# The first mixer as one stage, with its row norms applied late

## The chip, the cores and the metric

The kernel runs on one core of one Trainium2 chip. The metric is the device time of one execution in microseconds (us). The chip's engines are named as the profile names them: PE is TensorE (matrix products; PEld its weight loads), DVE is VectorE, ACT is ScalarE, POOL is GpSimd, and SP is the engine whose queue issues the transfers here. They run side by side, each through its own instructions in order, and wait for one another only by semaphores.

## The reference, cut to what matters

The program computes two transformer blocks over 512 tokens of width 1024. The change touches only the first mixer, which is the first thing computed. Everything behind it (the expert feed-forward of the first block, the whole second block) stays as it is.

```
h  = x + hybrid_mixer(rms_norm(x, mix_norm_g), w_in, ..., w_out)

x_lru, g_lru, a_glu, b_glu = split(n @ w_in)            # 4 x 512 columns
xc    = depthwise_conv(x_lru, width 4)
# per direction (forward, backward):
r, i  = sigmoid(block_diag(xc, w_r)), sigmoid(block_diag(xc, w_i))
log_a = 8 * r * log_sigmoid(lambda);  a = exp(log_a)
u     = sqrt(-expm1(2 log_a)) * (i * xc)
h_t   = a_t h_(t-1) + u_t                               # a scan along the tokens
y_lru = (h_fwd + h_bwd) * gelu(g_lru)
glu   = a_glu * sigmoid(b_glu)
c     = depthwise_conv(glu, width 31)
y_conv = silu(group_layer_norm(c))                      # groups of 64 channels
y     = concat(rms_norm(y_lru, beta_lru), rms_norm(y_conv, beta_conv))
out   = y @ w_out
```

## The kernel before, in words

All activations lie transposed, channels on the 128 partitions and the 512 tokens along the row, so that 1024 channels are 8 chunks of 128x512. A weight matrix is read in panels of 128x1024 (512 KB), which give one output chunk each: SP loads a panel into one of four ring slots (L231), ACT copies it half by half to a rounded high part (L240, L242), POOL subtracts to get the low part (L268), and PE sums 24 products of 128x512: high weight by high input (L282), high by low (L283), low by high (L289). Four PSUM banks take the outputs in turn. The same helper is used throughout the program. ACT's split of panel p+1 stands in its queue in front of its work on the output of panel p (`split_next`).

The mixer is a row of blocks of code, with a barrier of all engines between any two of them:

- `start`: SP loads constants, vectors, x and the first four panels of w_in. DVE squares x and sums the squares over the chunks (15 operations, L330 and L332).
- `norm_x`: PE sums over the partitions (L412), ACT takes the root (L400), DVE inverts it (L427) and scales the 8 chunks (L429), ACT rounds them (L448), and POOL and DVE make the low parts (L455).
- `hybrid_branches`, first block: PE multiplies by the 16 panels of w_in in the order x, gelu, glu, sigmoid, and ACT brings each output out of its bank with its function (L663). DVE runs the short convolution (L718, L720) and the product of the gated branch (L729) beside it. Then PE multiplies the 16 gates (L639; ACT's sigmoid L671), and convolves three of the four chunks of the long convolution by 31 products each with a diagonal matrix (L647), which POOL makes (L623) in 8 buffers. Beside it DVE makes the decay from a tanh with a reciprocal (L734 to L741, eight times, once for each chunk and direction), scans (L743, L745), multiplies by the gelu (L749, L752), and only then convolves the fourth chunk itself, 31 taps (L759, L761).
- second block: the group norm of the four convolved chunks (L779 to L808).
- two calls of `rms` (L398 to L455), one for each branch, one behind the other.
- `linear_add`: the 8 panels of w_out, each followed on DVE by the addition to x (L549) and the squares of the new x (L330, L332).

Behind it stand the next `norm_x` and the expert feed-forward, which are not changed.

Of the kernel before, what the change touches and what calls it, by code (L numbers as in the profile page):

```python
# [29 lines left out]
P = 128  # L30
T = 512
# [36 lines left out]
HALF = PANEL // 2  # L68

# [265 lines left out]
def start(m, io, ahead):  # L335
# [4 lines left out]
    with nc.Block() as block:  # L340
        @block.sync
        def _(sp):
            sp.dma_start(m.const[:, :], io["constants"]).then_inc(loaded, 16)
            sp.dma_start(m.vec[:, :], io["vectors"]).then_inc(loaded, 16)
            for k in range(4):
                sp.dma_start(m.x[:, 2 * k:2 * k + 2, :], io["x"][:, 2 * k:2 * k + 2, :]).then_inc(x_loaded[k], 16)
            sp.sem_inc(m.low, SLOTS)
            sp.sem_inc(m.half_low, SLOTS)
            for s, (source, width) in enumerate(ahead):
                load_panel(m, sp, s, s, source, width)  # L350
            sp.wait_ge(loaded, 32)

        @block.vector
        def _(dve):
            for c in range(DC):
                if c % 2 == 0:
                    dve.wait_ge(x_loaded[c // 2], 16)
                add_squares(m, dve, c)
# [8 lines left out]

        @block.scalar
        def _(act):
            split_high(m, act, (0, 0), 0)  # L370
# [192 lines left out]
def hybrid_mixer(m, io, ahead):  # L563

    with ExitStack() as ctx:
        space = Space(m, ctx, "hybrid", 29904)
        lru, conv = hybrid_branches(m, io, space, panels_ahead(io["w_out"]))
        rms(m, lambda c: lru[:, c, :], 0, lambda c: m.v("beta_lru", c), LRU_C4, T, space)
        rms(m, lambda c: conv[:, c, :], LRU_C4, lambda c: m.v("beta_conv", c), LRU_C4, T, space)
    linear_add(m, io["w_out"], ahead)  # L570


def hybrid_branches(m, io, space, ahead):
    nc = m.nc
# [9 lines left out]
    tanh = take(2 * C4, T)  # L584
    gate_i = take(2 * C4, T)
    root = take(2 * C4, T)
    inv = take(2 * C4, T)
# [4 lines left out]
    b_sig = conv  # L592

    side = m.sem("mix_side_loaded")
    first = m.panels
    in_evac = m.sem("mix_in_evacuated")
    lam_exp = m.sem("mix_lambda_exp")
    lam_done = m.sem("mix_lambda_done")
    xc_ready = m.sem("mix_xc_ready")
    glu_ready = m.sem("mix_glu_ready")  # L600
    gate_done = m.sem("mix_gate_products")
    gate_evac = m.sem("mix_gates_evacuated")
    tanh_done = m.sem("mix_tanh_done")
# [3 lines left out]
    conv_done = m.sem("mix_conv_evacuated")  # L607
    V = m.v
    with nc.Block() as block:
        @block.sync  # L610
        def _(sp):
            sp.dma_start(gate_w, io["lru_gates"]).then_inc(side, 16)
            weight_panels(m, sp, io["w_in"], 4 * C4, ahead)
# [3 lines left out]
        def _(pool):  # L617
            split_low(m, pool, 4 * C4)

            for k in range((C4 - 1) * CONF_TAPS):  # L620
                if k >= DIAGS:
                    pool.wait_ge(diag_used, k - DIAGS + 1)
                nc.gpsimd.tensor_scalar(diag[:, k % DIAGS, :], m.const[:, IDENT:IDENT + P],  # L623
                                        V("conf_w", k), None, ALU.mult).then_inc(diag_ready, 1)

        @block.tensor
        def _(pe):
            panel_products(m, pe, 4 * C4)

            pe.wait_ge(side, 16)  # L630
            pe.wait_ge(xc_ready, C4)
            for j in range(4 * C4):
                gate, way, c = j // (2 * C4), j // C4 % 2, j % C4
                if j >= 4:
                    pe.wait_ge(gate_evac, j - 3)
                else:

                    pe.wait_ge(in_evac, 4 * C4)
                nc.tensor.matmul(m.bank[j % 4][:, :], gate_w[:, (way * 2 + gate) * C4 + c, :], xc[:, c, :],  # L639
                                 start=True, stop=True).then_inc(gate_done, 1)  # L640


            pe.wait_ge(glu_ready, C4)
            for k in range((C4 - 1) * CONF_TAPS):
                c, tap = divmod(k, CONF_TAPS)
                pe.wait_ge(diag_ready, k + 1)
                nc.tensor.matmul(m.bank[4 + c][:, :], diag[:, k % DIAGS, :], glu_pad[:, c, tap:tap + T],  # L647
                                 start=(tap == 0), stop=(tap == CONF_TAPS - 1)).then_inc(diag_used, 1)

        @block.scalar  # L650
        def _(act):
            order = m.scalar_order

            order.step(act, nc.scalar.activation(lam[:, 0, :], m.vec[:, VEC["lam"]:VEC["lam"] + 8], ACT.Abs))
            nc.scalar.activation(lam[:, 1, :], lam[:, 0, :], ACT.Exp, scale=-1.0).then_inc(lam_exp, 1)
            kinds = [(x_pad, ACT.Copy, LRU_LEFT), (g_gelu, ACT.Gelu_apprx_tanh, 0), (glu_pad, ACT.Copy, CONF_LEFT),
                     (b_sig, ACT.Sigmoid, 0)]
            for j in range(4 * C4):
                dst, func, left = kinds[j // C4]
                out = dst[:, j % C4, left:left + T]  # L660
                split_next(m, act, first // SLOTS + j // SLOTS, j % SLOTS)
                act.wait_ge(m.used, used_count(first + j))
                order.step(act, nc.scalar.activation(out, m.bank[j % 4][:, :], func))  # L663
                act.sem_inc(m.bank_free[j % 4], 1)
                act.sem_inc(in_evac, 1)
            for j in range(4 * C4):
                gate, way, c = j // (2 * C4), j // C4 % 2, j % C4
                act.wait_ge(gate_done, j + 1)
                dst = tanh if gate == 0 else gate_i
                bias = V("b_rg" if gate == 0 else "b_ig", way * C4 + c)  # L670
# [2100 lines left out]
```

## Time and profile before

| | |
|---|---|
| time, median of 3 runs | 4083.49 us (4082.08 to 4089.62) |
| time of the profiled execution | 4088.65 us |
| its span, first to last instruction | 4086.9 us |
| PE busy | 3698.0 us, 90% |
| DVE, ACT, POOL busy | 2138.9, 1500.0, 1964.1 us |
| mean granted clock of PE | 0.944 of full |

A row of a timeline gives the start, the busy time, the engine, the line of the kernel, the operation, the tile written and those read with their shapes, and how many instructions were merged. Idle time before it and what ended it stand in brackets. All times are us from the start of the span unless marked ns.

### The profile page before, as it was taken

The page shows a single profiled execution, that of the slowest core. Times are in us where ns is not written, and L with a number is a line of the kernel's source. Part 1 is how long each engine was busy: PE and PEld are TensorE (multiplying, and loading weights), DVE is VectorE, ACT ScalarE, POOL GpSimd, SP SyncE. Part 2 cuts the span into 40 slices and gives each one's busy share as a digit, 9 for nine tenths or more (in the row PEclk, how much of TensorE's full clock was granted, in tenths as well). Part 3 has the DMA queues.
Part 4 walks back from the last instruction along what each step waited for, and adds up shares of the span by engine and source line. Part 5 has one row for each costly group of instructions (what it writes and reads, how often), then busy time and mean ns, then how long its engine had stood idle before and what let it go on. Part 6 is the DMA issues. An engine that isn't in the chain of part 4 may idle for free. (4 is left out here: it accounts for less than half of the span.)

```text
span 4086.9 us, 50848 instructions
## 1 busy us (share of the span) xinstructions
PE 3698.0 (90%) x17284; PEld 3080.0 (75%) x17284; DVE 2138.9 (52%) x3369; ACT 1500.0 (37%) x2617; POOL 1964.1 (48%) x1517
## 2 busy tenths in 40 slices
PE   6948999998899999999989885999979998589999
PEld 5526999998899999988867623788758886357887
DVE  4563398874999867653326126433333322654330
ACT  3322455663333333444223303343234422343332
POOL 3624477336788777655424201454435543114444
PEclk9978999999999999999999867999989999689999
DMA  3002355458999989533332200223323334202332
GB/s 114 24 11 82 105 167 164 167 224 318 357 406 405 365 334 344 180 97 98 92 104 85 62 0 23 90 92 94 88 64 95 96 95 94 56 16 87 95 91 91
DMA packets 172652, 569.68 MB, mean 139 GB/s; under 512 B 15457, under 2 KB 58593, under 8 KB 155012
## 3 DMA queue, kind: packets, MB, share of 16 engines
q1 hardware_dynamic: 152244, 427.68, 31.8%
q0 software_dynamic: 20304, 140.78, 9.2%
q8 instruction: 44, 0.72, 0.1%
q14 instruction: 60, 0.49, 0.0%
HBM read 518.33 MB, written 50.07 MB: 139 GB/s over the span
## 5 line engine op out<-in xcount | busy, mean ns | idle before, releaser
L268 POOL TENSOR_TENSOR weight_low<-weight_ring,weight_high 128x512 fp32r<-128x512 f32 x1264 | 1721.5, 1384 | 1731.7 <-ACT weight_high L240 1308.3
L282 PE MATMUL banks<-normed_high,weight_high 128*128 128x512 f32 (+1 forms) x2592 | 973.1, 375 | 85.6 <-PEq L391 43.9
L283 PE MATMUL banks<-normed_low,weight_high 128*128 128x512 f32 (+1 forms) x2592 | 964.8, 372 | 0.0
L240 ACT ACTIVATE weight_high<-weight_ring 128x512 fp32r<-128x512 f32 x632 | 398.8, 631 | 1328.1 <-PE banks L289 1226.1
L282 PEld LDWEIGHTS banks<-normed_high,weight_high 128*128 128x128 f32 x2592 | 496.5, 192 | 160.2 <-issue 76.7
L289 PE MATMUL banks<-normed_high,weight_low 128*128 128x512 f32 (+1 forms) x2592 | 588.6, 368 | 6.8 <-POOL weight_low L268 6.5
L283 PEld LDWEIGHTS banks<-normed_low,weight_high 128*128 128x128 f32 x2592 | 495.6, 191 | 63.9 <-issue 1.5
L289 PEld LDWEIGHTS banks<-normed_high,weight_low 128*128 128x128 f32 x2592 | 473.3, 188 | 71.7 <-POOL weight_low L268 10.5
L242 ACT ACTIVATE weight_high<-weight_ring 128x512 fp32r<-128x512 f32 (+1 forms) x632 | 389.3, 616 | 78.9 <-PE banks L289 77.7
L1740 DVE TENSOR_TENSOR square<-square,banks 128x512 f32<-128x512 f32 x88 | 60.5, 687 | 417.0 <-PE banks L289 415.4
L282 PE MATMUL banks<-parked_high,weight_high 128*128 128x384 f32 x768 | 262.2, 341 | 16.9 <-ACT weight_high L240 11.4
L283 PE MATMUL banks<-parked_low,weight_high 128*128 128x384 f32 x768 | 261.3, 340 | 0.0
L282 PE MATMUL banks<-hidden_high,weight_high 128*128 128x512 f32 x576 | 229.2, 398 | 0.0
L283 PE MATMUL banks<-hidden_low,weight_high 128*128 128x512 f32 x576 | 225.7, 392 | 0.0
L1762 DVE SCALAR_TENSOR_TENSOR residual<-banks,residual 128x512 f32<-128x512 f32 x32 | 22.1, 692 | 380.2 <-PE banks L289 380.2
L1243 DVE SCALAR_TENSOR_TENSOR picked_rows<-picked_rows,banks 128x1024 f32<-128x1024 f32 x128 | 155.5, 1215 | 54.4 <-DMA picked_rows<-in_expert_rows,picked_experts 53.8
L282 PE MATMUL banks<-middle_high,weight_high 128*128 128x512 f32 x448 | 180.3, 403 | 0.0
L283 PE MATMUL banks<-middle_low,weight_high 128*128 128x512 f32 x448 | 176.5, 394 | 0.0
L1249 DVE SCALAR_TENSOR_TENSOR banks<-picked_rows,picked_weight,banks 128x1024 f32<-128x1024 f32 x128 | 164.1, 1282 | 10.1 <-ACT picked_weight L1261 10.1
L282 PEld LDWEIGHTS banks<-parked_high,weight_high 128*128 128x128 f32 x768 | 145.8, 190 | 18.8 <-ACT weight_high L240 9.8
L1232 POOL DMA_INDIRECT picked_rows<-in_expert_rows,picked_experts x128 | 134.5, 1051 | 43.5 <-DVE banks L1249 25.3
L289 PE MATMUL banks<-parked_high,weight_low 128*128 128x384 f32 x768 | 151.9, 340 | 0.0
(360 smaller groups left out, 5666.9 us busy)
## 6 DMA issues: line engine op xcount, KB each, us to landing
weight_ring<-in_experts SPq DMA_DIRECT2D x256, 512.0 KB
weight_ring<-in_ffn_gate SPq DMA_DIRECT2D x88, 512.0 KB
weight_ring<-in_ffn_up SPq DMA_DIRECT2D x88, 512.0 KB
weight_ring<-in_ffn_down SPq DMA_DIRECT2D x64, 512.0 KB
expert_gates<-spread_space SPq DMA_DIRECT2D x6, 4096.0 KB, 12.2
parked_space<-expert_gates SPq DMA_DIRECT2D x24, 768.0 KB
parked_space<-parked_activations SPq DMA_DIRECT2D x24, 768.0 KB
weight_ring<-in_a_w_in SPq DMA_DIRECT2D x28, 512.0 KB
```

The costliest lines, as they stand in the source:

```text
L240: m.nc.scalar.activation(m.w_hi[:, s % PARTS, 0:HALF], m.ring[:, s, 0:HALF], ACT.Copy).then_inc(m.half_high, 1)
L242: m.nc.scalar.activation(m.w_hi[:, s % PARTS, HALF:width], m.ring[:, s, HALF:width], ACT.Copy).then_inc(m.high, 1)
L268: m.nc.gpsimd.tensor_tensor(m.w_lo[:, s % PARTS, at], m.ring[:, s, at], m.w_hi[:, s % PARTS, at].bitcast(FP), ALU.subtract).then_inc(done, 1)
L282: m.nc.tensor.matmul(out, w_hi, hi(c), start=(first and c == 0), stop=False)
L283: m.nc.tensor.matmul(out, w_hi, lo(c), start=False, stop=False)
L289: ins = m.nc.tensor.matmul(out, w_lo, hi(c), start=False, stop=(last and c == chunks - 1))
L1232: m.nc.gpsimd.indirect_dma_start(picked.rows[:, k % ROWS, :], None, io["expert_rows"], bass.IndirectOffsetOnAxis(ap=picked.expert[:, k:k + ...
L1243: m.nc.vector.scalar_tensor_tensor(out=halves[:, 0], in0=halves[:, 0], scalar=1.0, in1=picked.token, op0=ALU.mult, op1=ALU.mult, accum_out ...
L1249: m.nc.vector.scalar_tensor_tensor(out=picked.total, in0=halves[:, 1], scalar=picked.weight[:, k:k + 1], in1=picked.total, op0=ALU.mult, o ...
L1740: nc.vector.tensor_tensor(tile, tile, m.bank[2 * v + 1][:, :], ALU.mult).then_inc(product.sem, 1)
L1762: ins = nc.vector.scalar_tensor_tensor(out=x, in0=m.bank[c % 4][:, :], scalar=0.5, in1=x, op0=ALU.mult, op1=ALU.add)
```

## The change

The mixer becomes one block of code, from the loads to the additions to x.

- `start` keeps only the loads, in another order (vectors, two chunks of x, panel 0, the rest of x, panel 1, constants, panels 2 and 3), and what PE gives to the semaphores. The input of w_in is x times the gain, not yet divided by its norm: ACT rounds x*gain, and DVE makes the low part. DVE squares x behind that, PE sums over the partitions behind panel 1, ACT takes the root, DVE inverts it, and DVE multiplies each output of w_in by it as it takes it out of its bank.
- The panels of w_in come in the order glu and sigmoid of chunks 2, 3, 0, 1, then the four of x, then the four of gelu. ACT applies sigmoid and gelu in place, behind the split of the panel two further on.
- DVE convolves chunks 2 and 3 itself, 31 taps each, in pairs, and chunks 0 and 1 stay on PE (62 products, not 93). 20 of the 31 pairs stand between the outputs of w_in, two at a panel from the fifth on, one at each panel of x.
- The decay comes from an exponential on ACT. DVE's reciprocals and four other operations of each of the eight turns go.
- The steps of the group norm stand between the taps on PE and the recurrences on DVE.
- The two branch norms are late as well: w_out's input is the branch times beta. A half panel of w_out (`half_panel`) gives an output chunk of one branch, DVE multiplies it by that branch's inverse root and adds it to x. So there are 16 half outputs, two to a panel, and w_out is repacked on the host's side of the layout.

```diff
@@ start
         def _(sp):
-            sp.dma_start(m.const[:, :], io["constants"]).then_inc(loaded, 16)
+            sp.sem_inc(m.low, SLOTS)
+            sp.sem_inc(m.half_low, SLOTS)
             sp.dma_start(m.vec[:, :], io["vectors"]).then_inc(loaded, 16)
             for k in range(4):
                 sp.dma_start(m.x[:, 2 * k:2 * k + 2, :], ...).then_inc(x_loaded[k], 16)
+                if k == 0:
+                    load_panel(m, sp, 0, 0, *ahead[0])
             for s, (source, width) in enumerate(ahead):
-                load_panel(m, sp, s, s, source, width)
+                if s:
+                    load_panel(m, sp, s, s, source, width)
+                if s == 1:
+                    sp.dma_start(m.const[:, :], io["constants"]).then_inc(loaded, 16)
@@ hybrid_branches, TensorE
+            for j in range(IN):
+                s = j % SLOTS
+                pe.wait_ge(m.bank_free[s], fill0 + j // SLOTS + 1)
+                ready = (lambda c: pe.wait_ge(x_low, c + 1)) if j == 0 else None
+                part_products(...).then_inc(m.used, 1)
+                if j == 1:
+                    pe.wait_ge(loaded, 32)
+                    pe.wait_ge(prepared.sem, prepared.base + 1)
+                    scale.sums(pe)
...
+            def out_panel(k):
+                banks = [2 * k % SLOTS, 2 * k % SLOTS + 1]
+                for b in banks:
+                    pe.wait_ge(m.bank_free[b], out_fill0 + 2 * k // SLOTS + 1)
+                if k in (0, OUT // 2):
+                    pe.wait_ge(out_low, k + C4 if k else C4)
+                half_panel(m, pe, out_first + k, k % SLOTS, banks, 0 if k < OUT // 2 else C4)
+            gates()
+            taps(0, CONF_TAPS)
+            average(2)
+            average(3)
+            taps(CONF_TAPS, CONF_TAPS + 8)
+            square_sum(2)
+            square_sum(3)
+            taps(CONF_TAPS + 8, CONF_TAPS + 16)
+            average(0)
+            taps(CONF_TAPS + 16, PE_TAPS)
+            square_sum(0)
+            row_sum(0, lru_sq)
+            average(1)
+            out_panel(0)
+            square_sum(1)
+            for k in range(1, OUT // 2):
+                out_panel(k)
+            row_sum(1, sq)
+            for k in range(OUT // 2, OUT):
+                out_panel(k)
@@ hybrid_branches, ScalarE
+            act.wait_ge(loaded, 32)
+            for c in range(DC):
+                if c % 2 == 0:
+                    act.wait_ge(x_loaded[c // 2], 16)
+                nc.scalar.activation(m.n_hi[:, c, :], m.x[:, c, :], ACT.Copy, scale=V("mix_g", c)).then_inc(x_high, 1)
+                if c == 1:
+                    split_high(m, act, (0, 0), 0)
...
+            for j in range(IN + SHAPE_BEHIND):
+                if j < IN:
+                    split_next(m, act, first // SLOTS + j // SLOTS, j % SLOTS)
+                if j == 1:
+                    scale.root(act)
...
+                if j >= SHAPE_BEHIND and HYBRID_ORDER[j - SHAPE_BEHIND][0] in ("gelu", "sigmoid"):
+                    shape(shapes, *HYBRID_ORDER[j - SHAPE_BEHIND])
+                    shapes += 1
...
+            square_centred(2)
+            square_centred(3)
+            root_of(2)
+            root_of(3)
+            split_next(m, act, out_first // SLOTS, 0)
+            lru_input(0)
+            evacuate(0)
+            lru_input(1)
+            square_centred(0)
+            lru_input(2)
+            lru_input(3)
+            root_of(0)
+            evacuate(1)
+            square_centred(1)
+            row_root(0)
+            root_of(1)
@@ hybrid_branches, VectorE
+            for j in range(IN):
+                kind, c = HYBRID_ORDER[j]
...
+                dve.wait_ge(m.used, used_count(first + j))
+                order.step(dve, vec.tensor_tensor(dst, m.bank[j % 4][:, :], m.sum[:, :], ALU.mult))
+                dve.sem_inc(m.bank_free[j % 4], 1)
+                if kind in ("sigmoid", "gelu"):
+                    dve.sem_inc(scaled, 1)
+                if kind == "x":
+                    short_conv(c)
+                if j == 2:
+                    lambdas()
+                if j >= 4:
...
+                    more = 1 if kind == "x" else 2
+                    long_conv(taps, taps + more)
+                    taps += more
...
+            def recur(c):
+                for w in (c, C4 + c):
+                    dve.wait_ge(root_done, ways.index(w) + 1)
+                    order.step(dve, vec.scalar_tensor_tensor(out=root[:, w, :], in0=decay[:, w, :], scalar=1.0,
+                                                             in1=root[:, w, :], op0=ALU.add, op1=ALU.mult))
+                    order.step(dve, vec.tensor_tensor(root[:, w, :], root[:, w, :], gate_i[:, w, :], ALU.mult))
+                    turn = slice(None) if w < C4 else slice(None, None, -1)
+                    order.step(dve, vec.tensor_tensor_scan(gate_i[:, w, turn], decay[:, w, turn], root[:, w, turn], 0.0,
+                                                           ALU.mult, ALU.add))
...
+            def add_out(branch, o):
+                k = branch * OUT // 2 + o // 2
+                done = m.used if o % 2 else m.half_used
+                dve.wait_ge(done, used_count(out_first + k))
+                t = part[:, o % 2, :]
+                order.step(dve, vec.tensor_tensor(t, m.bank[o % 4][:, :], inv[:, branch, :], ALU.mult))
+                dve.sem_inc(m.bank_free[o % 4], 1)
+                order.step(dve, vec.tensor_tensor(m.x[:, o, :], m.x[:, o, :], t, ALU.add))
...
+            centre(2)
+            centre(3)
+            recur(0)
+            normalise(2)
+            recur(1)
+            lru_low(0)
+            normalise(3)
+            recur(2)
+            lru_low(1)
+            centre(0)
+            recur(3)
+            lru_low(2)
+            lru_low(3)
+            normalise(0)
+            centre(1)
+            row_inverse(0)
+            normalise(1)
+            add_out(0, 0)
+            add_out(0, 1)
+            for k, c in enumerate(gln):
+                conv_low(c)
+                add_out(0, 2 + k)
+            add_out(0, 6)
+            add_out(0, 7)
+            row_inverse(1)
+            for o in range(DC):
+                add_out(1, o)
+                add_squares(m, dve, o)
```

## Rows read from the trace of the kernel before

**Rows 1.** Windows by stage: length; busy of PE, PEld, DVE, ACT, POOL; clock, DMA share, GB/s.

```profile
0.00:39.00 39.00, 2.10 (x3) 0.57 (x3) 25.89 (x32) 9.75 (x15) 7.20 (x9) 1.00 0.34 119
39.00:128.40 89.40, 89.40 (x384) 73.57 (x384) 23.40 (x35) 31.20 (x51) 46.96 (x40) 1.00 0.35 106
128.40:143.20 14.80, 13.90 (x33) 6.19 (x33) 0.69 (x1) 10.83 (x16) 0.00 (x0) 1.00 0.00 0
143.20:223.30 80.10, 80.05 (x187) 34.97 (x185) 75.00 (x78) 12.71 (x22) 70.26 (x85) 1.00 0.00 0
223.30:237.40 14.10, 0.00 (x0) 0.00 (x0) 13.42 (x18) 0.68 (x1) 0.00 (x0) 0.67 0.00 0
237.40:262.60 25.20, 9.06 (x16) 3.76 (x16) 18.67 (x12) 9.27 (x14) 0.00 (x0) 0.70 0.00 0
262.60:297.90 35.30, 12.92 (x17) 4.93 (x17) 18.75 (x14) 12.13 (x20) 6.96 (x5) 0.60 0.00 0
297.90:344.20 46.30, 46.30 (x192) 37.75 (x192) 19.38 (x20) 9.73 (x16) 22.77 (x16) 0.94 0.30 91
```

**Rows 2.** Timeline of PE: two products at the low level, the gates, the taps.

```profile
39.53 0.63 PE L283 MATMUL banks<-normed_low,weight_high 128*128 128x512 f32 x1
39.95 0.63 PE L282 MATMUL banks<-normed_high,weight_high 128*128 128x512 f32 x1
...
129.44 13.97 PE L639 MATMUL banks<-hybrid_space 128*128 128x512 f32 x32 [0.90 <-ACTq L665]
143.24 80.01 PE L647 MATMUL banks<-hybrid_space 128*128 128x512 f32 x186
```

**Rows 3.** Timeline of the start, DVE and ACT, and transfers of its first 16 us.

```profile
8.91 0.69 DVE L330 TENSOR_TENSOR residual_squares<-residual 128x512 f32<-128x512 f32 x1 [8.91 <-DMA residual<-in_x]
...
13.98 0.63 ACT L240 ACTIVATE weight_high<-weight_ring 128x512 fp32r<-128x512 f32 x1 [11.60 <-DMA weight_ring<-in_w_in]
...
23.02 3.35 DVE L427 RECIPROCAL norm_space<-norm_space 128x512 f32<-128x512 f32 x1 [3.25 <-ACT norm_space L400]
...
0.00:16.00 16.00, 0.00 (x0) 0.00 (x0) 6.79 (x10) 2.43 (x3) 0.19 (x4) 1.00 0.82 283
```

**Rows 4.** Timeline of DVE, first and last of the tiny operations on lambda.

```profile
40.43 0.85 DVE L701 TENSOR_SCALAR hybrid_space<-hybrid_space 128x8 f32<-128x8 f32 x1 [1.53 <-ACT hybrid_space L655]
...
45.99 0.17 DVE L711 TENSOR_SCALAR hybrid_space<-hybrid_space 128x8 f32<-128x8 f32 x1
```

**Rows 5.** Lines, ns min/median/max: taps beside the low split, alone; POOL's split beside taps.

```profile
L720 DVE SCALAR_TENSOR_TENSOR hybrid_space<-hybrid_space,vectors x12: 737/748/1780, 68.0 to 79.5; 128x512 f32<-128x512 f32 x12
...
L761 DVE SCALAR_TENSOR_TENSOR hybrid_space<-hybrid_space,vectors x30: 751/752/753, 213.7 to 236.6; 128x512 f32<-128x512 f32 x30
...
L268 POOL TENSOR_TENSOR weight_low<-weight_ring,weight_high x6: 1342/1579/1734, 64.9 to 77.3; 128x512 fp32r<-128x512 f32 x6
...
74.18:79.62 5.44, 5.44 (x25) 4.50 (x24) 5.41 (x6) 1.75 (x4) 3.31 (x2) 1.00 0.34 98
```

**Rows 6.** Timeline: ACT's eight tanh; one turn of DVE's recurrence.

```profile
144.23 5.01 ACT L677 ACTIVATE hybrid_space<-hybrid_space 128x512 f32<-128x512 f32 x8
...
159.18 0.68 DVE L740 TENSOR_TENSOR hybrid_space<-hybrid_space 128x512 f32<-128x512 f32 x1
159.90 0.74 DVE L741 TENSOR_TENSOR hybrid_space<-hybrid_space 128x512 f32<-128x512 f32 x1
160.67 1.28 DVE L743 TENSOR_TENSOR_SCAN hybrid_space<-hybrid_space 128x512 f32<-128x512 f32 x1
```

**Rows 7.** Timeline of DVE beside w_out: first addition, a slow sum, the last sum.

```profile
306.16 0.69 DVE L549 TENSOR_TENSOR residual<-residual,banks 128x512 f32<-128x512 f32 x1 [8.89 <-PE banks L289]
307.00 0.87 DVE L330 TENSOR_TENSOR residual_squares<-residual 128x512 f32<-128x512 f32 x1
...
313.34 1.67 DVE L332 TENSOR_TENSOR residual_squares<-residual_squares,square 128x512 f32<-128x512 f32 x1
...
345.88 0.69 DVE L332 TENSOR_TENSOR residual_squares<-residual_squares,square 128x512 f32<-128x512 f32 x1
```

More of the change, by code:

```diff
@@ L68 @@
 HALF = PANEL // 2
+HYBRID_ORDER = [(kind, c) for c in (2, 3, 0, 1) for kind in ("glu", "sigmoid")] + \
+               [(kind, c) for kind in ("x", "gelu") for c in range(LRU_C4)]
 VEC = {}
@@ L566, in hybrid_mixer, with half_panel @@
         space = Space(m, ctx, "hybrid", 29904)
[L567 to L570, printed above, removed]
+        hybrid_branches(m, io, space, ahead)
+def half_panel(m, pe, p, s, banks, chunks):
+    half = HALF // P
+    ready = ((m.half_high, m.half_low), (m.high, m.low))
+    for k in range(2):
+        out = m.bank[banks[k]][:, :]
+        high, low = ready[k]
+        pe.wait_ge(high, p + 1)
+        for c in range(half):
+            w_hi = m.w_hi[:, s % PARTS, (k * half + c) * P:(k * half + c + 1) * P]
+            m.nc.tensor.matmul(out, w_hi, m.n_hi[:, chunks + c, :], start=(c == 0), stop=False)
+            m.nc.tensor.matmul(out, w_hi, m.n_lo[:, chunks + c, :], start=False, stop=False)
+        pe.wait_ge(low, low_count(p))
+        for c in range(half):
+            w_lo = m.w_lo[:, s % PARTS, (k * half + c) * P:(k * half + c + 1) * P]
+            ins = m.nc.tensor.matmul(out, w_lo, m.n_hi[:, chunks + c, :], start=False, stop=(c == half - 1))
+        ins.then_inc(m.used if k else m.half_used, 1)
 def hybrid_branches(m, io, space, ahead):
@@ L583, in hybrid_branches @@
     xc = take(C4, T)
-    tanh = take(2 * C4, T)
+    root = take(2 * C4, T)
     gate_i = take(2 * C4, T)
-    root = take(2 * C4, T)
-    inv = take(2 * C4, T)
+    decay = take(2 * C4, T)
     conv = take(C4, T)
@@ L2704, in layouts @@
     io["x"] = f["x"][0].T.reshape(DC, P, T).transpose(1, 0, 2)
-    io["w_in"] = panels(f["w_in"][0])
-    io["w_out"] = panels(f["w_out"][0])
+    kinds = ("x", "gelu", "glu", "sigmoid")
+    w = panels(f["w_in"][0])
+    io["w_in"] = np.stack([w[kinds.index(kind) * LRU_C4 + c] for kind, c in HYBRID_ORDER])
+    w = panels(f["w_out"][0])
+    io["w_out"] = np.stack([np.concatenate([w[2 * k, :, half], w[2 * k + 1, :, half]], axis=1)
+                            for half in (slice(0, HALF), slice(HALF, PANEL)) for k in range(DC // 2)])
     gates = np.zeros((P, 4 * LRU_C4, P), np.float32)
```

405 lines of the change are left out of this document (240 added, 165 removed).

## The prediction, made before the changed kernel ran

> **What bounds the kernel now.** I read the windows by stage first, because the page's shares (PE 90% busy) are an average over a long program and say little of this stage. [rows 1] shows where the mixer's time lies. Up to 39 us nothing but the first norm runs; PE is busy 2.1 us. From 39 to 128.4 PE is full with w_in. From 143.2 to 223.3 PE is full with taps and DVE is 75 of 80 us busy with the recurrences. Then come four stretches in which PE waits for DVE and ACT: DVE's own 31 taps to 237.4, the group norm to 262.6, two branch norms to 297.9, with PE at 0, 9.1 and 12.9 us. Last come the eight panels of w_out to 344.2. DVE is idle for three quarters of w_in (23.4 of 89.4 us). So the stage is bound by PE and DVE in turn, and most work of one has none of the other beside it. Then I read PE's and DVE's timelines for the price of each operation.
>
> **The units.** A panel of w_in or w_out is 24 products, 5.44 us at full clock by the window of one panel [rows 5]. At the low level (1.2 GHz) two products start 0.42 us apart [rows 2], 10.2 us a panel. A gate or tap is 0.86 us of PE (80.01/93; the 186 records are two a tap) [rows 2]. On DVE a dependent tap costs 0.79 us alone (0.752 busy and some 0.03 for its semaphore), a pair of which only the second is waited for 1.54 [rows 5]; a product of two tiles 0.73 (159.18 to 159.90) [rows 6]; one that takes a bank with its semaphores 0.84 (306.16 to 307.00) [rows 7]; a reciprocal 3.39 [rows 3]. I lay the new code out in the time of the old trace.
>
> **Start.** ACT and DVE wait for the constants, which SP now issues behind six transfers of 512 KB. 283 GB/s over 16 us are 4.5 MB [rows 3], and everything issued is 4.5 MB, the constants end at 3.5 MB of it. Panel 0 landed at 13.98 with 3.0 MB ahead or in it. So the constants land between 12.5 and 16 us; I take 14.5. ACT rounds two chunks and panel 0 (0.55 to 0.6 us each), PE begins at 17.4, and runs one chunk for each low part of DVE (0.78 us) or at the low level, 0.85 us: panel 0 to about 26, panel 1 to 31.5. DVE has its 8 low parts at 23, then 15 squares and sums, 11 us, and 2 us lost to POOL (below): 36. Here the change adds a wait: PE, behind panel 1, stands until 36 for `prepared`, and panels 2 to 15 are queued behind it. The sum over partitions takes 1 to 2 us, so panel 2 starts at 37.5. 14 panels at 5.44 end at 114, where before w_in ended at 128.4: **14 us less**. If the wait of 4.5 us lets the clock fall, panel 2 costs up to 2.7 us more (the first panel of w_out took 8.1 at its low start, 297.9 to 306); if squares and constants are early, it is 4.5 less. DVE's inverse, banks 0 and 1 and the tiny operations on lambda (5.7 us, [rows 4]) are done at 50, before panel 4 ends at 54.
>
> **DVE beside w_in.** From panel 4's end DVE owes, clean: 4.8 us for the fifth output (with two gated products and two pairs), 3.9 or 4.7 for the next three, 6.1 for the first x (0.85, four short taps 2.95, one gated product, one pair), 5.3 for three more, 3.9 for each gelu. Up to the last bank's product it is 52.0 us, and 0.7 of waiting for the sigmoid, which ACT gives only behind the next split. POOL's split takes some away: 12 taps beside it had a median of 748 and a maximum of 1780 ns [rows 5], and six operations filled a panel's 5.44 us, where six clean ones are 4.49. So DVE loses 0.95 us a panel, 10.5 in 11 panels. 63.2 us behind 53.8 the last output is out of its bank, at 117.3, 3.3 behind PE. It never holds PE up, since four banks allow three panels of lag, nor ACT, whose gelu comes two panels behind. Bounds: no loss, 2.8 us earlier; a loss of a whole pair of POOL's operations a panel is a rival.
>
> The Trainium skill (SBUF — State Buffer, "Who interferes with whom") has a rule that speaks against this: GpSimd and a DVE operation with two SBUF inputs hold their shared ports for a whole instruction, and the other blocks fully. By it the 20 pairs would pay up to POOL's full time, as in rival B. The rows agree in kind (1780 against 748) and show less in the mean.
>
> **Gates and taps.** ACT's last gelu and a load of sigmoid's table end near 120, PE has four gates ahead and 12 to go at 0.86: 131, before it was 143.2 (here 2 us of the 14 are given back). DVE's other 11 pairs (17 us) and 8 products end at 144.5, ACT's exponential, tanh and root (8 each at 0.63 [rows 6], and up to three table loads) at 150. Both are hidden, for PE does chunk 0's taps first, 31 x 0.86 = 26.7, to 157.7, and the averages of chunks 2 and 3 stand behind them. DVE is idle from 144.5 to 158.7: this cover costs 14 us of DVE and is late next.
>
> **The DVE chain.** From 158.7 DVE is never free. Two centrings 1.6; four recurrences, each of two turns of 0.82+0.78+1.30 [rows 6] and two products, 7.25, so 29.0; two of the group norm's inversions 4.1 each; three or four low parts and a centring 4. That is 43 us, to 202. The eight turns before were 7.68 us each (61 us), with 31 taps (24) and the norms behind. PE's other 31 taps and sums (34 us) end at 189 under it and then wait.
>
> **Into w_out.** ACT's last branch input, the row sum, chunk 1's average: PE starts w_out at 205, panel 0 at the low level first, 8.1 us: 213. The square sum of chunk 1 stands behind it, its root comes at 214.7, and DVE, which has waited, normalises to 218.8. Then eight additions of branch 0 at 1.57 and four low parts, 15.6, and 2 of POOL's: 236.5. PE in turn waits for banks 0 and 1 (to 221.4, 2 us) and does panels 2 and 3 to 232.4, the row sum 3.4, ACT's root: 236.7. DVE inverts to 240.2. Branch 1 owes 0.84 + 3 x 0.73 = 3.03 us of DVE for each output, against 2.72 of PE: 8 of these less the first sum are 23.5, and 2 for POOL (one sum here took 1.67 and not 0.69 [rows 7]), so **265.7**, 9 us behind PE's last product. DVE, not PE, ends the stage.
>
> **Sum.** Before, the last sum ended at 345.88+0.69 = 346.6. The saving is 346.6-265.7 = 80.9 us; nothing behind it changes. The profiled execution took 4088.65 (span 4086.9), so 4007.8 in its terms. It was 5.2 over the median of the runs, 4083.49, and in the median's terms the time is 4002.6: I predict 4003.
>
> **Rivals.**
> - C, everything is hidden: no wait for the squares (-4.5), no port loss (-2.8 in w_in, -4 behind). 4003-11 = 3992. For it: DVE's taps alone were never slowed (751 to 753). Against: POOL splits in every panel.
> - A, w_out at the low level throughout. For it: PE's clock was 0.60 to 0.70 in all three stretches with gaps [rows 1], and w_out now has gaps of 2 to 4 us. Against: it rose within w_out before. 8 panels at 10.2 from 205, the sums at double price: 296 and 3 for the last output; 299-265.7 = 33 more, 4036.
> - B, DVE loses each of POOL's operations whole. Two at 1.34 or more a panel [rows 5] leave 2.8 of 5.44 us. The 52.7 us then take 101 and not 63.2, ACT's gelu and so the gates wait for it; w_out's six splits add 10: +48, 4051. Against it: six operations in a panel.
> - D, slower than before: the same lock hits every DVE operation, not every POOL one. On the path are 23 operations at the start, 68 beside w_in, 51 beside w_out, 142. At the longest seen, 1.03 us extra each, they cost 146, of which 18 are counted above: 4003+128 = 4131. It turns slower from 99/142 = 0.70 us extra for each, a mean of 1.45. The mean seen beside w_out is 1.04, on one operation in three.
>
> **How the numbers follow.** The forecast 0.70, C 0.12, A 0.08, B 0.06, D 0.03, something else 0.01. The terms of the forecast can move by: constants -2 to +1.5, clock behind the wait 0 to +2.7, wait -4.5 to 0, port loss -7 to +8, the semaphores' 0.03 to 0.1 on some 140 operations -2 to +8. I give 3986 to 4030, which holds C. 0.2% (8 us) is what a measurement can tell here; faster by that 0.96, within it 0.01, slower 0.03.
>
> **What would show it.** Right: w_in's last product near 114, gates to 131, a DVE gap of some 14 us before the first centring near 159, w_out's first product near 205 and last near 257, the last sum near 266, the next norm as before. Wrong: L268's pair above 3.3 us a panel and DVE more than four panels behind (B), products 0.42 us apart in w_out's later panels (A), no idle PE behind panel 1 (C). I am wrong altogether if DVE's wait before the centring is gone, for then the chain starts late and every later term shifts.

## The result, and the profile after

The changed kernel took 4014.45 us (median of 4 runs, 4008.59 to 4017.76) against 4083.97 of the kernel before (median of 4 runs, one more than in the table above); the ratio is 0.9826, 95% interval 0.9809 to 0.9843, which is 64 to 78 us less. On a second chip it took 4017.84 (5 runs, 4010.01 to 4025.06) against 4085.7, again 0.9826. The forecast was 4003, with 3986 to 4030 as its range. The profiled execution took 4008.59 us, its span was 4006.8.

The windows by stage of the changed kernel, in the columns of [rows 1], cut where its own stages end:

```profile
0.00:37.70 37.70, 17.66 (x50) 11.81 (x51) 21.22 (x27) 10.92 (x16) 9.77 (x10) 1.00 0.53 192
37.70:116.10 78.40, 78.40 (x339) 64.56 (x338) 65.29 (x83) 25.48 (x40) 44.47 (x34) 0.98 0.30 88
116.10:138.00 21.90, 17.33 (x33) 6.90 (x32) 20.89 (x31) 12.53 (x18) 0.00 (x0) 0.84 0.00 0
138.00:165.60 27.60, 27.60 (x65) 12.12 (x65) 7.92 (x13) 17.54 (x27) 21.32 (x31) 1.00 0.00 1
165.60:212.10 46.50, 38.12 (x82) 16.00 (x81) 43.97 (x44) 10.50 (x18) 25.46 (x27) 0.89 0.06 23
212.10:263.50 51.40, 49.26 (x204) 37.69 (x202) 47.27 (x47) 21.09 (x32) 17.25 (x12) 1.00 0.22 62
263.50:272.10 8.60, 0.00 (x0) 0.00 (x0) 7.80 (x12) 0.00 (x0) 0.00 (x0) 0.70 0.00 0
```

DVE, 23.4 us busy beside w_in before, is 65.3 of 78.4 us busy there now. The three stretches in which PE stood for DVE and ACT are gone. What is left behind w_in are 8 us in which PE stands in front of w_out and some 20 us in which DVE stands in front of the first centring. The mixer's last sum ended at 346.6 us before and ends at 272.0 now, 74.5 us earlier; the forecast was 80.9 earlier. A mark here is the time, from the start of the span, at which a named operation begins or ends. These rows of DVE's timeline carry the marks: the wait at the start, the last bank product of w_in, the gap before the first centring, and the last sum.

```profile
39.02 3.35 DVE L480 RECIPROCAL residual_squares<-residual_squares 128x512 f32<-128x512 f32 x1 [1.60 <-ACT residual_squares L474]
...
120.89 0.69 DVE L958 TENSOR_TENSOR hybrid_space<-banks,residual_squares 128x512 f32<-128x512 f32 x1
...
140.91 5.18 DVE L1032 TENSOR_TENSOR hybrid_space<-hybrid_space 128x512 f32<-128x512 f32 x8
165.59 1.47 DVE L980 SCALAR_TENSOR_TENSOR hybrid_space<-banks,hybrid_space 128x512 f32<-128x512 f32 x2 [19.50 <-PE banks L725]
...
271.35 0.69 DVE L335 TENSOR_TENSOR residual_squares<-residual_squares,square 128x512 f32<-128x512 f32 x1
```

And on PE's timeline: the sum of the squares and the first products behind it at the low level, the gates, the first taps.

```profile
37.18 1.10 PE L468 MATMUL banks<-residual_squares,constants 128*128 128x512 f32 x2 [3.14 <-DVEq L894]
37.71 0.90 PE L285 MATMUL banks<-normed_high,weight_high 128*128 128x512 f32 x1
38.41 0.63 PE L286 MATMUL banks<-normed_low,weight_high 128*128 128x512 f32 x1
38.84 0.63 PE L285 MATMUL banks<-normed_high,weight_high 128*128 128x512 f32 x1
...
115.90 1.88 PE L704 MATMUL banks<-hybrid_space 128*128 128x512 f32 x4
117.94 1.10 PE L704 MATMUL banks<-hybrid_space 128*128 128x512 f32 x2 [0.16 <-DVEq L959]
121.78 1.10 PE L704 MATMUL banks<-hybrid_space 128*128 128x512 f32 x2 [2.75 <-DVEq L959]
124.55 13.45 PE L704 MATMUL banks<-hybrid_space 128*128 128x512 f32 x24 [1.67 <-ACT hybrid_space L803]
137.83 26.78 PE L713 MATMUL banks<-hybrid_space 128*128 128x512 f32 x62
```

**How far a time can be read.** From w_in's last product on, the marks of this kernel repeat to 0.1 us: on the second chip it had its last sum at 272.10. Not everything in front does: there the constants landed 1.2 us earlier and PE's sum of the squares began at 36.0 and not 37.2, but the products behind it ran at the low level for longer, and w_in ended at the same 116.06. Two kernels below whose code is the same up to the gates (the two of experiment 4) ended w_in 0.55 us apart, so a difference of half a microsecond between two marks is not read as an effect. The span behind the last sum varies more. It was 3740.3 us before, 3734.8 here, 3751.1 in the second profile of the same kernel, and 3733 to 3751 over all kernels below, whose code there is the same. So a median can differ by some 5 us from what the stage says: here it is 69.5 us less (4083.97 to 4014.45) against 74.5 of the stage. This is not scatter alone. In 11 of the 13 comparisons on record the median fell by less than the last sum moved, by 3 us on average over all 13. A part of it lies directly behind the mark: the first panel of the next stage ended 25.7 us behind the last sum before, and 26.3 to 27.5 us behind it in all other kernels. The rest is not explained. In the experiments the end of the last sum is the measure and the median stands beside it.

### The profile page after: what moved, and what is told of

It reads as the page before. It is cut to its first block and busy times, and to the rows that moved or that the text cites. A ratio compares the mean times of both kernels' runs of the same rounds, so it can differ in the third digit from the quotient of the medians.

```text
span 4006.8 us, 50694 instructions
## 1 busy us (share of the span) xinstructions
PE 3671.6 (92%) x17222; PEld 3065.6 (77%) x17222; DVE 2155.2 (54%) x3409; ACT 1502.4 (37%) x2618; POOL 1926.6 (48%) x1478
## 5 line engine op out<-in xcount | busy, mean ns | idle before, releaser
L285 PE MATMUL banks<-normed_high,weight_high 128*128 128x512 f32 (+1 forms) x2528 | 948.2, 375 | 72.6 <-ACT weight_high L243 31.0
L286 PE MATMUL banks<-normed_low,weight_high 128*128 128x512 f32 (+1 forms) x2528 | 939.1, 371 | 0.0
L285 PEld LDWEIGHTS banks<-normed_high,weight_high 128*128 128x128 f32 x2528 | 483.4, 191 | 145.0 <-issue 63.7
L292 PE MATMUL banks<-normed_high,weight_low 128*128 128x512 f32 (+1 forms) x2528 | 574.1, 368 | 7.1 <-POOL weight_low L271 6.8
L286 PEld LDWEIGHTS banks<-normed_low,weight_high 128*128 128x128 f32 x2528 | 483.2, 191 | 61.3 <-issue 1.8
L292 PEld LDWEIGHTS banks<-normed_high,weight_low 128*128 128x128 f32 x2528 | 462.3, 188 | 70.0 <-POOL weight_low L271 10.7
L1993 DVE TENSOR_TENSOR square<-square,banks 128x512 f32<-128x512 f32 x88 | 60.5, 688 | 417.0 <-PE banks L292 415.4
L1485 POOL DMA_INDIRECT picked_rows<-in_expert_rows,picked_experts x128 | 134.7, 1052 | 41.8 <-DVE banks L1502 23.4
## 6 DMA issues: line engine op xcount, KB each, us to landing
expert_gates<-spread_space SPq DMA_DIRECT2D x6, 4096.0 KB, 12.4
```

The lines of the kernel that those rows point to most:

```text
L285: m.nc.tensor.matmul(out, w_hi, hi(c), start=(first and c == 0), stop=False)
L286: m.nc.tensor.matmul(out, w_hi, lo(c), start=False, stop=False)
L292: ins = m.nc.tensor.matmul(out, w_lo, hi(c), start=False, stop=(last and c == chunks - 1))
L1485: m.nc.gpsimd.indirect_dma_start(picked.rows[:, k % ROWS, :], None, io["expert_rows"], bass.IndirectOffsetOnAxis(ap=picked.expert[:, k:k + ...
L1993: nc.vector.tensor_tensor(tile, tile, m.bank[2 * v + 1][:, :], ALU.mult).then_inc(product.sem, 1)
```

## The experiments

All but one start from the changed kernel. The first run repeated it. The edits are shown cut to the lines that matter.

> The changed kernel once more, as the measure for the others of this chip. In its first trace the mixer's last sum ended at 272.0 us and DVE stood idle for 19.5 us before the first centring at 165.6. Expected: the same marks within 1 us and a median between 4008 and 4018.

Measured: last sum 272.10, first centring at 165.64 behind 19.52 us, median 4017.84. The marks held; the span was 4023.2, for the reason above.

**1. Whose wait is the gap of 19.5 us?**

```
-            taps(0, CONF_TAPS)
+            taps(0, 8)
             average(2)
             average(3)
-            taps(CONF_TAPS, CONF_TAPS + 8)
+            taps(8, 24)
             square_sum(2)
             square_sum(3)
-            taps(CONF_TAPS + 8, CONF_TAPS + 16)
+            taps(24, CONF_TAPS + 8)
             average(0)
-            taps(CONF_TAPS + 16, PE_TAPS)
+            taps(CONF_TAPS + 8, PE_TAPS)
```

> The averages of chunks 2 and 3 stand behind the 8th tap of PE and not behind the 31st, and their square sums behind the 24th. Theory (the order on PE holds DVE back): DVE has its convolution at 141 us and ACT its first root at 152, so the recurrences begin at 152 and not at 167, the chain behind them moves as a whole until PE's taps (195.5) bound it, and the mixer ends 12 to 15 us earlier, near 259. Rival (PE and POOL have no less to do, and their 62 taps bound the stage anyway): the end moves by less than 4 us.

DVE's timeline of this kernel at the same place:

```profile
141.03 5.18 DVE L1032 TENSOR_TENSOR hybrid_space<-hybrid_space 128x512 f32<-128x512 f32 x8
146.25 1.29 DVE L980 SCALAR_TENSOR_TENSOR hybrid_space<-banks,hybrid_space 128x512 f32<-128x512 f32 x2
152.26 0.69 DVE L991 SCALAR_TENSOR_TENSOR hybrid_space<-hybrid_space 128x512 f32<-128x512 f32 x1 [4.73 <-ACT hybrid_space L851]
...
259.02 0.69 DVE L335 TENSOR_TENSOR residual_squares<-residual_squares,square 128x512 f32<-128x512 f32 x1
```

The gap is gone, the first recurrence waits for ACT's root and begins at 152.3 as computed, and the last sum ends at 259.7, **12.4 us earlier**; median 4005.06. The theory held. 15 us were won at the recurrences and 12.4 kept: PE's taps end at 195.5, its sums follow without a gap, and w_out begins at 200.25, which is PE's bound.

**2. Is the wait for the squares worth anything?**

```
-                if j == 1:   # in two places: PE's sums, ACT's root
+                if j == 2:
```

> PE's sum of the squares and ACT's root of it stand behind panel 2 of w_in and not behind panel 1. Theory (the wait for the squares and the low clock behind it are a real loss): PE does not stand from 33.9 to 37.2, panel 3 begins 5 us earlier, w_in's last product ends at 111 and not 116, and since DVE then starts a little late the mixer ends 3 to 4 us earlier. Rival (DVE is what bounds w_in, PE's gain is lost in DVE's lag): last product 5 us earlier, but the last bank's product by less than 1.5, and the end by less than 1.5.

w_in's last product ended at 110.4 and not 116.1, 5.7 us earlier, but the last bank product only 2.4 (119.2), and the last sum 2.3 (269.8); median 4010.79. That lies between the two: DVE's lag behind PE (from w_in's last product on PE to the last bank product on DVE) rose from 5.5 to 8.8 us and ate more than half. Each theory had a part of it.

**3. Who ends the mixer?**

```
-                add_out(1, o); add_squares(m, dve, o)
+                add_out(1, o)                      # ACT: m.square[o % 2] = x[o]^2
+                if o > 1: add_square(o - 1)        # DVE: m.sum += m.square, one output later
```

> In branch 1 of w_out ACT squares the new x, and DVE only adds the square of the output before. Theory (DVE bounds the end of the mixer, 8.6 us behind PE's last product at 263.5): eight operations of 0.73 us leave DVE, and the end moves from 272.0 to about 267, where PE's last product begins to bound. Rival (the new waits between DVE and ACT cost what they save): less than 1.5 us.

Last sum 267.9, 4.2 us earlier, median 4007.86. DVE is the bound at the end; of the 5.8 us taken from it 4.2 were kept. It still is: PE's last product ended at 263.1, 4.8 us before the last sum, and not at the 267 that the expectation named as PE's bound.

**4. What is the placement of the taps under w_in worth?**

```
-                    more = 1 if kind == "x" else 2
+                    more = 0
```

> All 31 pairs of DVE's taps stand behind w_in; the rest is the changed kernel. Theory (PE's order gives the first centring, the placement under w_in is covered by it): DVE's last bank product comes at 117 and not 121.6, 31 pairs at 1.46 us end at 163, PE's gates end 4.6 us earlier and its first 31 taps at 160, so the first centring moves from 165.6 to 168 or 169 behind the eight products, and the mixer ends 2 to 4 us later. Rival (20 pairs hidden under w_in are worth their 29 us, less DVE's idle 19.5): 10 us later or more. Against the kernel before this stays some 70 us faster.

The last bank product came at 117.4, PE's averages at 163.9, the first centring at 168.9, and the last sum at 273.6: **1.5 us later**, median 4013.74. So 40 of DVE's 62 long taps could leave w_in for 1.5 us. The work was hidden in w_in, but what it won was not needed: DVE then stood in front of the average for 19.5 us. The rival's arithmetic (29 us less 19.5) leaves out two things: 4 of the 40 taps stood behind the last bank product already, and that product came 4.2 us earlier. The other 36 taps at 0.73 us, less 4.2 and 19.5, are 2.6 us (an estimate from these rows), and the first centring came 3.3 us later.

> Both the early averages and all of DVE's taps behind w_in. The placement of the taps cost 1.5 us with the averages behind tap 31 (mixer end 273.6 against 272.1). Theory (there it was covered by PE's order): with the averages early the cover is gone, DVE's convolution is ready at 163, the first centring stands at 168 and not at 146, and the end goes back to 271 to 274, so the same edit now costs 12 to 14 us. Rival (the placement is free anyway, DVE's earlier gates pay for it): 262 or less.

With the averages early the same edit cost **20.2 us** (279.9 against 259.7, median 4025.27), and this kernel is slower than the changed one. The direction was the theory's, the size was not. PE's timeline has the reason:

```profile
130.16 7.03 PE L713 MATMUL banks<-hybrid_space 128*128 128x512 f32 x16
162.18 3.78 PE L725 MATMUL banks<-hybrid_space,constants 128*128 128x512 f32 x4 [24.98 <-DVEq L950]
165.75 14.94 PE L713 MATMUL banks<-hybrid_space 128*128 128x512 f32 x32
```

The average waits for DVE 25 us with 54 taps queued behind it, 46 us of PE's work that needs nothing of it. I had priced the wait by DVE's chain alone. In the first kernel of this experiment, with the averages behind the 31st tap, the same wait was 6.4 us.

**5. Gates shaped one panel behind and not two.**

```
-    SHAPE_BEHIND = 2
+    SHAPE_BEHIND = 1
```

> SHAPE_BEHIND is 1 and not 2: ACT's sigmoid and gelu stand one panel behind. Theory: ACT waits for DVE's bank product, which is 5 us late at the four gelu panels, so the split of the last panel or two comes 1 us late; the sigmoids come earlier and spare DVE 0.4 us; the mixer ends within 2 us of 272.0. Rival (ACT's wait throttles PE at each of these panels): w_in's last product 5 us later or more, and the end with it.

Last sum 272.10, the same to the last digit as in the repeated run; last bank product 121.66 against 121.58; median 4011.82. This part of the change is worth nothing either way.

**6. What do POOL's operations cost DVE?** POOL subtracts 32 of 512 columns of each half and leaves the rest of the low part at zero, so this kernel leaves out most of the correction by the low weights.

```
-            split_low(m, pool, IN)     # and OUT
+            small_low(m, pool, IN)     # slice(0, 32), slice(HALF, HALF + 32)
```

> POOL makes only 32 of 512 columns of each low half in the panels of w_in and w_out (the rest of the low parts is left at zero, so these two products lack most of their low weight part); PE's work is the same. It takes away POOL's collisions with DVE. Theory (DVE waits for POOL's operations): DVE's last bank product comes within 1 us of PE's last product (now 5.5 behind), the recurrences lose 4 us of stretching between 189 and 197, and w_out's additions 5 us: the mixer ends 13 to 17 us earlier, at 255 to 259. Rival (the waits are hidden by PE): less than 5 us. By my blind estimate of the lock it is 2.8 and 4 us.

The last sum ended at 251.5, **20.6 us earlier**, more than the theory's 13 to 17; median 3996.5. The same lines with and without the collisions, first the changed kernel's scans and its groups beside w_out:

```profile
L995 DVE TENSOR_TENSOR_SCAN hybrid_space<-hybrid_space x8: 1224/1274/2169, 168.5 to 206.4; 128x512 f32<-128x512 f32 x8
...
L1027 DVE TENSOR_TENSOR residual<-residual,hybrid_space 128x512 f32<-128x512 f32 x16 | 14.1, 880 | 2.5 <-DVE hybrid_space L1025 2.5
L1011 DVE SCALAR_TENSOR_TENSOR normed_low<-hybrid_space,vectors,normed_high 128x512 fp32r<-128x512 f32 x4 | 5.8, 1438 | 0.1
```

then those of the kernel with small low parts:

```profile
L1007 DVE TENSOR_TENSOR_SCAN hybrid_space<-hybrid_space x8: 1223/1249/1278, 153.0 to 187.6; 128x512 f32<-128x512 f32 x8
...
L1039 DVE TENSOR_TENSOR residual<-residual,hybrid_space 128x512 f32<-128x512 f32 x16 | 11.1, 692 | 2.5 <-DVE hybrid_space L1037 2.5
L1023 DVE SCALAR_TENSOR_TENSOR normed_low<-hybrid_space,vectors,normed_high 128x512 fp32r<-128x512 f32 x4 | 3.0, 752 | 0.1
```

Where the 20.6 us lie, by marks of the two kernels: w_in's last product 7.9 earlier (116.1 to 108.2), most of it at the start, where POOL splits three panels beside DVE's low parts and squares (the sum of the squares began at 30.9 and not 37.2, or 36.0 in the repeated run, whose constants landed as early as here); DVE's lag behind it 5.5 to 0.8 us, 4.7; PE's gates, no longer waiting, 2.9 more to the first centring (165.6 to 150.1); and 5.1 in the chain and w_out.

Not all of it is time that an engine spent longer in an operation. Between panel 4 and the last bank product DVE ran the same 68 operations in 60.5 us of busy time and in 47.7, which is 12.9 us. At the start a part is the clock: PE stood 2.5 us before the sum of the squares and not 3.1 (4.9 in the repeated run), and the products behind it ran 0.23 us apart and not 0.43. The operations that were stretched read no bank; the twelve bank products took 0.692 us on average in both kernels. So DVE and POOL hold each other up without a semaphore between them, and the sentence of the first section that engines wait for one another only by semaphores does not hold for these two.

**7. The three edits of 1 to 3 together.**

> The three edits of the runs before together: averages early, sums behind panel 2, squares on ACT. Alone they ended the mixer 12.4, 2.3 and 4.2 us earlier. Theory (each stands in another stretch of one chain): they add, and the mixer ends at 253, the median about 19 us under that of the changed kernel. Rival (with the averages early PE's taps bound the chain, and one of the others is lost): 256 or later.

Last sum 252.05, 20.05 earlier, where the three alone sum to 18.9; median 3994.99 (ratio 0.9773, 0.9759 to 0.9786). They add, and none is lost.

**8. A better balance.** Same as 7, with 16 pairs of taps under w_in:

```
-                    more = 1 if kind == "x" else 2
+                    more = 2 if j < 8 else 1
```

> The three edits together, and 16 pairs of DVE's taps under w_in and not 20 (two at each of the first four panels, then one). With the three edits PE's taps bound the stage, and PE's gates wait for DVE's last bank product, 8 us behind PE. Theory (this lag is what is left): the last bank product comes at 112 and not 118.4, PE's gates end at 127 and not 134.5, w_out begins at 189 and not 196.6, and the mixer ends at 244 to 246 and not 252.1. Rival (fewer taps hidden leave DVE later, and it binds): 250 or later.

The rival won: last sum 251.98, nothing gained; median 3991.98. The gates did end early (128.95 for 134.5), but PE then stood 3.5 us before its average, and DVE 5.7 us before the root of the square sum, which PE gives only behind its 24th tap:

```profile
128.78 7.03 PE L713 MATMUL banks<-hybrid_space 128*128 128x512 f32 x16
139.33 2.88 PE L725 MATMUL banks<-hybrid_space,constants 128*128 128x512 f32 x4 [3.52 <-DVEq L956]
142.00 14.75 PE L713 MATMUL banks<-hybrid_space 128*128 128x512 f32 x32
```

**9. The order mended once more.**

```
-            taps(0, 8)
+            taps(0, 16)
             average(2)
             average(3)
-            taps(8, 24)
+            taps(16, 24)
```

> The balanced kernel, with PE's averages of chunks 2 and 3 behind the 16th tap and not the 8th; the square sums stay behind the 24th. There PE stood 3.5 us before the average, DVE then 5.7 us for the first root of the group norm, and nothing was gained (mixer end 252.0 against 252.1). Theory (the wait of PE for DVE and then of DVE for PE gave back the earlier gates): PE has no gap, the square sums start at 151 and not 156.6, the first of DVE's group-norm inversions at 154 and not 158.3, w_out begins at 192 and not 196.5, and the mixer ends at 247 to 248. Rival (the early gates are worth nothing, DVE's chain is bound elsewhere): 251 or later.

```profile
130.04 13.90 PE L713 MATMUL banks<-hybrid_space 128*128 128x512 f32 x32
143.78 1.88 PE L725 MATMUL banks<-hybrid_space,constants 128*128 128x512 f32 x4
145.50 7.03 PE L713 MATMUL banks<-hybrid_space 128*128 128x512 f32 x16
152.37 1.88 PE L731 MATMUL banks<-hybrid_space,constants 128*128 128x512 f32 x4
```

No gap on PE, DVE's first inversion of the group norm at 154.05, w_out at 192.31, last sum at 247.74, all as forecast (the square sums began 1.4 us later than forecast); median **3989.9** us (5 runs, 3984.22 to 3991.42; ratio to the kernel before 0.9765, 0.9752 to 0.9779). This kernel beats both: 24.4 us of the mixer under the changed one. It does so although its gates ended 1.3 us later than in experiment 8, with the same code up to there and nearly the same waits. The two kernels' last 24 gate records, experiment 8 first:

```profile
118.41 10.54 PE L704 MATMUL banks<-hybrid_space 128*128 128x512 f32 x24 [1.67 <-ACT hybrid_space L803]
...
117.97 12.23 PE L704 MATMUL banks<-hybrid_space 128*128 128x512 f32 x24 [1.67 <-ACT hybrid_space L803]
```

PE had stood 0.63, 1.28 and 1.67 us between its gates in the one and 0.57, 1.29 and 1.67 us in the other. The granted clock over 118.0 to 121.5 was 1.00 in the one and 0.53 in the other.

**10. One part alone on the kernel before:** the decay by ACT's exponential.

```
-  inv = 1/(tanh+1); decay = 2*inv-1; root = root*inv     # DVE, 3 more ops and a reciprocal
+  decay = Exp(lam6 * r)                                  # ACT; DVE: root = (decay+1)*root
```

> The kernel before with one part of the change alone: the decay comes from ACT's exponential, and DVE loses its eight reciprocals and the small operations about them (7.68 us a turn to about 3.6, 33 us in all). Theory (PE's 93 taps run beside it to 223.3 and cover the rest): DVE's own taps end at 215, the group norm starts at 224.5 and not 237.9, with PE's clock still high, and the mixer ends near 331 and not 346.6: 13 to 16 us less for 33 us of DVE's work. Rival (DVE is the bound of the stage throughout): 30 us less.

In each turn a reciprocal and three other operations go (not four, as the list of the change has it) and one comes. A turn took 3.35 us and not 7.68, 34.6 us less for DVE in all; the last sum ended at 329.7, 16.9 us earlier, and the median is 4073.51 (ratio 0.9972, 0.9962 to 0.9981). DVE's own taps ended at 210.1 and DVE then stood until 225.5, because PE's 93 taps ran to 223.3. Half of what left DVE was covered by PE. So one sixth to a quarter of what the change saves can come from this part alone, by the medians (11.4 of 69.5) and by the mark (16.9 of 74.5). The rest comes with the taps and the norms moved as well. How it divides between them is not shown: no run here has the new block with the norms applied early, or the late norms in the old blocks.

## Why the prediction was right, and by how much it was off

Mark by mark, forecast and measured:

| mark | forecast | measured |
|---|---|---|
| ACT's first operation on x (constants there) | 14.5 | 13.9 |
| squares summed | 36 | 37.0 |
| w_in's last product | 114 | 116.1 |
| last bank product of w_in | 117.3 | 121.6 |
| gates end | 131 | 138.0 |
| first centring | 158.7 | 165.6 |
| end of the chain (last low part of branch 0) | 202 | 210.7 |
| first product of w_out | 205 | 212.1 |
| branch 0 added | 236.5 | 243.7 |
| last sum | 265.7 | 272.0 |

- **Start: held.** PE stood for the squares as forecast. The bound named for the clock came about: PE was idle from 34.0 to 37.2, and of the next eight products all but the first ran 0.43 us apart, until 41.4, at the low level, about 2 us in all. I had taken zero of the possible 2.7. Experiment 2 shows that more than half of what is won there does not come through. Earlier constants did not help either: in the repeated run PE's sum of the squares began 1.2 us earlier and w_in ended no earlier.
- **DVE beside w_in: the step that was mis-sized.** From panel 4's end (56.26) to the last bank product took 65.3 us, where 52.7 were clean: a loss of 12.6 us and not 10.5. This is what made the lag behind PE 5.5 and not 3.3. Experiment 6 confirms the size: 12.9 us on the same operations. What failed was the price per panel read from one panel's six operations [rows 5], 0.95 us; it was 1.15. The sample decides: all twelve short taps of the kernel before took 12.3 us on its timeline, where twelve at 0.748 are 9.0, and that is 1.5 us for each 5.44. The Trainium skill (SBUF — State Buffer, "Who interferes with whom") says that the operation that comes second waits out the first. The traces agree in kind: single taps took up to 1784 ns for 752, and a pair of POOL's up to 3.58 us for 2.54; both sides pay, and neither by its full partner each time (1.15 us of DVE in the mean beside a pair of 2.54).
- **Gates: a term left out.** The lag made PE wait twice for DVE's last bank products (2.75 us and 0.16) and then 1.67 us for ACT, whose last gelu waited for DVE too. Behind these waits the first gates ran at the low level (granted clock 0.50 over 124.6 to 127.3, 0.58 to 131.0, then 1.00): 24 records took 13.45 us, where 24 took 10.54 without the wait (experiments 4 and 6). I had priced the wait and not what it does to the clock. It is 2.9 us of the 7.0 by which the gates ended late; the rest is the late start and the lag. Experiments 8 and 9 show that shorter waits lower the clock in one profile and not in another, so this term is uncertain by some 2 us (12.23 against 10.54). The gates of the kernel with small low parts, on PE's timeline:

```profile
108.03 3.59 PE L716 MATMUL banks<-hybrid_space 128*128 128x512 f32 x8
111.96 10.54 PE L716 MATMUL banks<-hybrid_space 128*128 128x512 f32 x24 [0.33 <-ACT hybrid_space L815]
```

- These three make the 6.9 us of the first centring. **Behind it the sums held**: 26.8 us of taps, a chain of 45 for 43 us, w_out to the last sum 59.9 for 60.7. The last is in part luck, for two of its terms were off and cancelled. The forecast had w_out's first panel at the low level, 8.1 us, and it ran at full clock in 5.9. From the first addition to the end of branch 0 DVE took 19.5 us and not 17.7, for POOL's collisions cost more than the 2 us counted. (The forecast's "34 us" for PE's other taps and sums does not fit its own 157.7 and 189; it was 31, as measured, and nothing else uses it.) The cover I named, DVE's idle time before the centring, was 19.5 us and not 14, and experiment 1 shows that it was the cheapest thing to win.
- **Collisions behind w_in:** 4 us were counted, all beside w_out, and between 189 and 197 one recurrence was stretched by POOL's split of w_out's first two panels (a scan of 2169 ns), which I had not foreseen. So the chain took 45.1 us and not 43, although DVE's inversions and low parts in it were each as priced.
- **The rivals.** A (w_out at the low level) did not happen: PE's clock was 1.00 from 212.1 to its last product at 263.5. B and D overrated the lock: experiment 6 puts nearly all of it at 20.6 us, where B asked for 48 above what the forecast already held. B's sign came half: single pairs of POOL's passed 3.3 us (up to 3.58), but their mean from panel 4 on was 3.10, and DVE was one panel behind and not four. C was 11 us off the forecast on the other side; what it names (no loss to POOL, no wait) exists, but needs other code.
- **The forecast of the time.** The median is 11.5 us over the forecast of 4003, and the mixer's last sum 6.3 us over its mark. The other 5 us lie in what the forecast put at nothing ("nothing behind it changes"): the medians gave back that much of the mark's gain, and the runs explain only the 0.6 us of it that lies directly behind the mark.

## What to carry to other kernels

When two engines take turns, price every wait with what is queued behind it on its own engine: an average that waits 25 us for DVE in front of 54 taps that don't need it made the mixer end 20.2 us later, where DVE's chain alone had been priced at 12 to 14. Work hidden under another stage is worth only what the next wait lets through: 40 taps under w_in were worth 1.5 us with one order on PE and 20.2 with another. So lay out the marks of all engines first, then move the one instruction that waits.

## What was not expected of the hardware

- A short wait of PE can cost twice: behind 2.75 and 1.67 us of idle time between gates the next ones ran at the lower of the two levels (granted clock 0.84 over 116.1 to 138.0), and the 24 records took 13.45 us and not 10.54. Behind 1.3 and 1.67 us at the same place they took 10.54 in one kernel's profile and 12.23 in another's.
- Making POOL's long subtractions short was worth 20.6 us of a stage of 272 with no instruction fewer on any engine. Beside one of them a two-input operation of DVE took as much as 1.78 us and not about 0.75, and a scan 2.17 and not 1.22. An operation with one tile as its input was not safe either: in the kernel before, four of them (L718) took 0.54 to 1.52 us beside POOL's subtraction.
- The part of the program that no kernel here touches varied by 18 us from one profile to another (3733 to 3751), while the marks of the first stage, from w_in's last product on, repeated within 0.1 us for one kernel. Why, these runs do not show.
